# Hybrid decoder step on one core: the final norm beside the last eight expert slots

## The reference

```python
def rmsnorm(x, w):
    y = x * lax.rsqrt(jnp.mean(x * x, axis=-1, keepdims=True) + NORM_EPS)
    return y * w

# gsel = best group of the token, top_i = its two best experts in the group
eid = gsel[..., None] * EXPERTS_PER_GROUP + top_i
gate = jnp.sum(jax.nn.one_hot(eid, N_EXPERTS) * tw[..., None], axis=-2)
for e in range(N_EXPERTS):
    he = jax.nn.silu(h @ p['expert_w_gate'][e]) * (h @ p['expert_w_up'][e])
    y = y + gate[..., e:e + 1] * (he @ p['expert_w_down'][e])
x = x + y
# after the layer
y_prompt, y_sample = rmsnorm(x, norm_final)
```

## Time and profile before

| | us |
|---|---|
| median of three runs (lowest, highest) | 1233.64 (1231.39, 1235.2) |
| the profiled execution | 1233.92 |
| its span, first to last instruction | 1232.2 |
| TensorE busy | 1162.6 (94%) |
| POOL busy | 567.2 (46%) |
| DVE busy | 525.3 (43%) |
| ACT busy | 336.9 (27%) |

### The profile page before, as it was taken

The page is one execution under the profiler, slowest core; times in us unless marked ns, Lnnn a source line. Parts: engine busy times, 40 slices in busy tenths (PEclk is TensorE's granted clock), DMA queues, the critical chain, the costliest instruction groups (busy, mean ns, idle before and its releaser), DMA issues. The chain is left out here.

```text
span 1232.2 us, 31435 instructions
## 1 busy us (share of the span) xinstructions
PE 1162.6 (94%) x12690; PEld 830.3 (67%) x12690; DVE 525.3 (43%) x1250; ACT 336.9 (27%) x785; POOL 567.2 (46%) x821
## 2 busy tenths in 40 slices
PE   7999999999999999999999999689999999999990
PEld 6788878756656677787754545367777777777760
DVE  5466986644394425645523113532222222222223
ACT  5002012352441244564433222201111111111114
POOL 7512221110750248788632021046666666666661
PEclk9999999999999999999999999899999999999995
DMA  7401120134104110000075214499999897998838
GB/s 214 103 1 36 36 69 18 36 103 117 48 19 95 51 21 17 23 16 17 20 240 186 82 69 137 131 357 374 317 373 341 256 373 238 290 374 254 274 51 298
DMA packets 142874, 187.12 MB, mean 152 GB/s; under 512 B 39464, under 2 KB 89247, under 8 KB 142778
## 3 DMA queue, kind: packets, MB, share of 16 engines
q1 hardware_dynamic: 126010, 164.87, 39.6%
q0 software_dynamic: 15936, 20.57, 8.0%
q10 hardware_dynamic: 832, 0.33, 0.1%
HBM read 156.41 MB, written 29.32 MB: 151 GB/s over the span
## 5 line engine op out<-in xcount | busy, mean ns | idle before, releaser
L526 PE MATMUL ps<-hT,w_in 128*128 128x352 f32 (+1 forms) x624 | 192.6, 464 | 1.8 <-ACT cb L816 1.2
L526 PEld LDWEIGHTS ps<-hT,w_in 128*128 128x128 f32 x624 | 116.4, 190 | 66.5 <-issue 4.1
L3129 POOL DMA_INDIRECT sum_rows<-slot_out,scatter_rows x76 | 121.9, 1604 | 38.9 <-POOL scatter_rows L3128 26.1
L3261 DVE TENSOR_TENSOR slot_T<-slot_raw_T,vecs 128x256 f32<-128x256 f32 x75 | 32.8, 438 | 209.4 <-PE ps L3174 208.2
L3174 PE MATMUL ps<-qkv,slot_T 128*32 128x256 f32 x1920 | 109.9, 379 | 3.7 <-DVE slot_T L3261 2.5
L3174 PEld LDWEIGHTS ps<-qkv,slot_T 128*32 128x32 f32 x1920 | 74.8, 110 | 32.9 <-DVE slot_T L3261 4.8
L3106 POOL DMA_INDIRECT gathered<-h_rows,gather_rows x79 | 83.5, 1057 | 19.3 <-issue 12.2
L3218 ACT ACTIVATE slot_silu<-ps 128x128 f32<-128x128 f32 x77 | 21.5, 279 | 223.7 <-PE ps L3174 221.5
L3174 PE MATMUL ps<-cb,slot_T 128*32 128x256 f32 x1408 | 80.6, 379 | 0.0
L3174 PEld LDWEIGHTS ps<-cb,slot_T 128*32 128x32 f32 x1408 | 55.4, 110 | 20.5
L3224 ACT ACTIVATE slot_out<-ps,slot_weights 128x256 f32<-128x256 f32 x76 | 36.1, 475 | 112.6 <-PE ps L3185 112.6
(11 more groups left out here) (765 smaller groups left out, 2369.7 us busy)
## 6 DMA issues: line engine op xcount, KB each, us to landing
qkv<-in_expert_w_gate SPq DMA_DIRECT2D x6, 2048.0 KB
qkv<-in_expert_w_up SPq DMA_DIRECT2D x6, 2048.0 KB
qkv<-in_expert_w_down SPq DMA_DIRECT2D x6, 2048.0 KB
cb<-in_expert_w_gate SPq DMA_DIRECT2D x5, 2048.0 KB
cb<-in_expert_w_up SPq DMA_DIRECT2D x5, 2048.0 KB
zg<-in_expert_w_down SPq DMA_DIRECT2D x5, 2048.0 KB
third_w_down<-in_expert_w_down SPq DMA_DIRECT2D x5, 2048.0 KB
w_in<-in_w_in SPq DMA_DIRECT2D x18, 512.0 KB, 5.1
```

Of the source, the lines that this page charges most:

```text
L526: last = pe.matmul(pbank(b)[:, c, 0:n], w[:, k, :], hT[:, k, c * CH:c * CH + n], start=(k == 0), stop=(k == KD - 1))
L3129: pool.indirect_dma_start(quarter_sums, bass.IndirectOffsetOnAxis(ap=sidx[:, r:r + 1], axis=0), y[r][:], None, compute_op=ALU.add).then_in ...
L3261: dve.tensor_tensor(xT[:], xr[:], bc(nf, 2, ROWS_SLOT), ALU.mult).then_inc(s.xT, 1)
```

## The change

- The slots are split into early ones and the **last eight** (`LATE`). In this input these are slots 68 to 75, of which 74 and 75 hold no token. They all belong to the last four experts, one of each group, so that no token is in two of them.
- Early slots work as before. When all their adds have landed, SP loads the nine tiles of `sum_rows` (into buffers of their own, one of them the constants' masks), and ACT, POOL, DVE and SP norm and store them while the last slots are computed. The order is written out slot by slot: `ahead` and `behind` for ACT, `norms_ahead` and `norms_behind` for DVE.
- The scale of a row is computed by POOL, as (mean square + eps) to the power -0.5 (`scale`), and no longer by ACT with logarithm and exponential. ACT keeps the silu's table.
- The results of the last eight slots aren't added in DRAM. ACT evicts each as before, and SP moves its four quarters with four plain on-chip transfers into token rows (`to_rows`; tiles `last_out_0` and `last_out_1`, four slots each). POOL gathers the sums so far of these tokens (`sums`), POOL and DVE add them (`add_sums`), they are normed, and POOL writes them with indirect DMAs over the rows of `y_prompt` and `y_sample` (`last_out`, `last_sample_out`), after the plain stores of the tiles have landed.
- The token numbers for these transfers are computed by DVE ahead of its loop over slots (new L3436 to L3441).
- The norm's weights are loaded behind the third expert's. TensorE has 20 warm-up products in place of 16. The routing writes three numbers of rounds in place of six.

The core of the diff:

```diff
+                    for c in range(4):
+                        sp.dma_start(last_y[i // RING][c4[i % RING], c * QD:c * QD + QD], y[i % RING][c4[c]]).then_inc(moved[i], 16)
+                to_rows(0)
+                to_rows(1)
+                store(NT)
+                to_rows(2)
+                store(0)
+                store(1)
+                store(2)
+                to_rows(3)
+                store(3)
+                store(4)
+                store(5)
+                to_rows(4)
+                store(6)
+                to_rows(5)
+                to_rows(6)
+                to_rows(7)
+                store(7)
...
+                def scale(t):
+                    pool.wait_ge(f.sq, nth[t])
+                    pool.tensor_scalar(mean[:, t:t + 1], mean[:, t:t + 1], NORM_EPS, None, ALU.add).then_inc(f.eps, 1)
+                    pool.wait_ge(f.eps, nth[t])
+                    pool.tensor_tensor(rstd[:, t:t + 1], mean[:, t:t + 1], minus_half[:], ALU.pow).then_inc(f.rstd, 1)
...
+                scale(4)
+                pool.wait_ge(f.o0, 16)
+                sums(1)
+                pool.wait_ge(f.o1, 16)
+                sums(0)
+                last_rows(first + RING + 3, 3, n + 2)
+                scale(5)
+                scale(6)
+                scale(7)
+                add_sums(0)
+                scale(TILES)
+                pool.wait_ge(f.norm, 1)
+                pool.wait_ge(f.os, 16)
+                last_sample_out(0)
...
+                pool.wait_ge(f.out, 16 * (NT - 3))
+                last_out(0)
+                scale(TILES + 1)
+                pool.wait_ge(f.norm, 2)
+                last_out(1)
+                last_sample_out(1)
+                pool.wait_ge(f.late, 16 * 4)
...
+                ahead = {2: (1,), 3: (4,), 4: (7,)}
+                behind = {1: (NT, 0), 2: (2, 3), 3: (5, 6), 7: (TILES, TILES + 1)}
+                for i in range(LATE):
+                    if i < LATE - 1:
+                        silu(first + i + 1, hidden=True)
+                    for t in ahead.get(i, ()):
+                        mean_square(t)
+                    last_rows(i, first + i, n)
+                    for t in behind.get(i, ()):
+                        mean_square(t)
...
+                for i in range(LATE):
+                    dve.tensor_scalar(row_f[c4[i % RING], i // RING:i // RING + 1], route.token[c4[0], ds(first + i, 1)], 0.25, None, ALU.mult)
...
+                norms_ahead = {3: (NT,), 4: (2,), 5: (5,)}
+                norms_behind = {3: (0, 1), 4: (3, 4), 5: (6,), 6: (7,)}
```

More of the change, by code:

```diff
@@ L62 @@
 MOE_SEMS = "g0 g1 g2 d0 d1 d2 r0 r1 r2 r3 st ix xg xTp xT gu silu he hT down acc y0 y1 y2 y3".split()
-FIN_SEMS = "w x0 x1 x2 x3 x4 x5 x6 x7 x8 ones rstd y out".split()
+FIN_SEMS = "w x0 x1 x2 x3 x4 x5 x6 x7 x8 idx part0 part1 sum sq eps rstd y norm o0 o1 o2 os out late m0 m1 m2 m3 m4 m5 m6 m7".split()
 GATE_PE = {"columns": 1, "transposes": 2, "sums": 3, "rows": 4}
@@ L3087, in _ @@
                 sp.wait_ge(s.xg, 1)
-                for j in range(2, NE):
+                load(2)
+                sp.dma_start(wrow[:], A["norm_final"].partition_broadcast(P)).then_inc(f.w, 16)
+                for j in range(3, NE):
                     load(j)
-                landed = [sp.value_load(route.first[0:1, NE + 4 + r:NE + 5 + r], min_val=32 * NE // RING, max_val=16 * SLOTS // RING) for r in range(RING)]
-                sp.wait_ge(s.gu, bound(sp, NE - 2))
-                sp.dma_start(wrow, A["norm_final"].partition_broadcast(P)).then_inc(f.w, 16)
+                landed = early_landed(sp)
@@ L3101, in _, with store @@
-                sp.wait_ge(f.out, 16 * TILES)
+                    sp.wait_ge(out_y[r], landed)
+                for t in [NT] + list(range(NT)):
+                    sp.dma_start(tile_of[t], sum_rows[t * P:t * P + (P if t < NT else NS), :]).then_inc(x_in[t], 16)
+                first = early_slots(sp)
+                def store(t):
+                    sp.wait_ge(f.y, nth[t])
+                    dst = O["y_prompt"][0, t * P:t * P + P, :] if t < NT else O["y_sample"].rearrange("b t d -> (b t) d")
+                    sp.dma_start(dst, tile_of[t]).then_inc(stored_of(t), 16)
@@ L3103, in _ @@
+                sp.wait_ge(f.out, 16 * (NT - 3))
+                sp.wait_ge(f.late, 16 * 4)
             @block.gpsimd
```

219 lines of the change are left out of this document (149 added, 70 removed).

## The result

The changed kernel takes 1235.72 us, median of 20 runs (1233.43 to 1238.83); the kernel before took 1232.36 in 20 runs on the same chip. The ratio is 1.0021, 95% interval 1.0011 to 1.003. The forecast was 1227 and faster. The difference is within the 0.3% that the forecast took for no change, the time above its range of 1221.5 to 1235. None of these runs was in a slow state; the ratio is a little under that of the two medians, 1.0027.

What follows compares the result with a forecast made beforehand. TensorE bounds the kernel until the last expert slot, then a serial tail of 31.9 us. Span end 1223.2, plus 1.9 at the start and 1.72 beyond the span, gives 1226.8, said as 1227, against 1233.92; range 1221.5 to 1235.

Steps and rivals of the forecast that it cites:

- Loads, squares, norms beside the slots at no cost: Slots 68 to 75: the early tiles' loads, squares and norms fit into the engines' gaps; cost zero.
- The last product held up by norm 5: Last down product on TensorE: waits behind DVE's norm 5 for POOL's scale, 4.2 us late, the largest new cost.
- That product lasts 1.93 us: TensorE's last down product: keeps the earlier trace's 1.93 us, running from 1202.5 to 1204.4.
- Twelve issues of 0.43 us, 5.2 in all: SP's list behind ACT's last real output: three groups of four row moves, 0.43 us each, 5.2 us.
- From the scatter of the first half to the last scatter, 4.4 us: Tail from 1214.7 to 1219.1: POOL's scatter 1.06, scale 0.8, norm 1.3, two scatters at 1.06 us.
- From the last scatter to the end, 4.1 us: End of the span: scatters issued by 1219.1, down at 1222.8, 0.4 us for the last waits, end 1223.2.
- its own signs of being wrong: TensorE gaps in slots 69 to 72, POOL's power over 1 us, or last product to end not near 19 us.
- The start, +1.9: Between third row transpose and slot loop: DVE's added one-column instructions and drains cost 1.2 to 2.6 us, taken as 1.9.
- Warm-up at zero: Ahead of the first slots: the four added warm-up products run while TensorE waits for rows; cost zero.
- POOL and DVE get in each other's way: Rival: POOL's one-column instructions wait for whole norms at three scales, up to 3.7 us: 1230.5; chance 0.15.
- Slow power: Rival: POOL's power makes scales slow in slots 71, 72 and the tail; at 3 us each, 1239; chance 0.10.
- Late tiles: Rival: slot 67's scatter lands late, loads start 7.3 us later, TensorE loses 5.9: 1232.9; chance 0.12 including queue.

Runs made afterwards that it cites:

- e1: The changed kernel without POOL's closing wait for the four late scatters to land; ratio 1.0008 to the kernel before.
- e3: The changed kernel with DVE computing the late slots' token numbers before the first slot's rows arrive; ratio 1.0001 to the kernel before.
- e6: The changed kernel with 16 warm-up products instead of 20; ratio 1.002 to the kernel before.
- e9: The changed kernel without POOL's last two scatters and the waits for them; run once, stage length 422.9 us against 426.7.
- e12: The changed kernel with one added drain behind POOL's last gather, where POOL is idle; ratio 0.9999 to the kernel before.
- e2: The changed kernel with norm 5 moved behind slot 73's transposes; ratio 1.0015 to the kernel before.
- e10: e8 with an added drain behind POOL's last gather; ratio 0.9946 to the kernel before.
- e8: The changed kernel with the edits of e1, e2, e3 and e6, stores 5 and 7 reordered, slot 75's moves on ACT; ratio 0.9971 to the kernel before.
- e4: The changed kernel with two of the four row moves of slots 73 to 75 issued from ACT's queue; ratio 1.0019 to the kernel before.
- e11: e8 with ACT's moves ahead of its square and POOL's second-half scale ahead of its first-half scatter; ratio 0.9952 to the kernel before.
- e5: The changed kernel with a drain added behind POOL's last scale, ahead of the last scatters; run once, stage length 424.9 us against 426.7.
- e13: e8 with both the drain of e10 and the edits of e11; 1225.29 us, ratio 0.9934 to the kernel before.

## Why the prediction was wrong

It said 7.1 us less, and that the span would end at 1223.2 + 1.9 = 1225.1; it ended at 1233.1, 8.0 later. The steps in order, each against its own number:

- *Loads, squares, norms beside the slots at no cost*: right. TensorE lost 0.26 us up to slot 73's gate products; the down product behind them comes 0.5 us late. One tile landed too late for its square, by 1.18 us, and the slack took it.
- *The last product held up by norm 5*: right in place and cause. It started at 1204.23, where the forecast has 1204.4, but that closeness is partly luck: counted from the stage's start it is 397.9 us against 396.8. The hold-up is 5.6 us instead of 4.2 in this trace, and 4.6 in seven others with the same order (e1, e3 to e6, e9, e12). The store of tile 0 was issued 386.6 us into the stage (1192.94), behind SP's moves of slot 70; the forecast, with the start's 1.9, has even the store of tile 1 at 385.8. The forecast also took 0.48 us from the transpose to TensorE's start, but that pause in the earlier trace rows was ended by ACT's eviction; here it is 0.11 us (1204.12 to 1204.23).
- *That product lasts 1.93 us*: mis-sized. The price is from a row in which TensorE had waited 0.85 us ahead of it. Behind 6.42 us of waiting the products took 3.64, at the granted clock of 0.50: +1.7 us. e2, with 1.17 us of waiting and a granted clock of 1.00, shows 1.93.
- *Twelve issues of 0.43 us, 5.2 in all*: mis-sized. From the first issue to store 7 it is 1216.23 - 1208.68 = 7.55 us, 0.6 each: +2.35. The row it was from was a transfer of 16 KB. The range had 0.6 as its upper end, from loads of 512 KB. e2 shows that the end follows this list and not TensorE's last product. Eight of the twelve issues move the rows of slots 74 and 75, which hold no token in this input; a list without them was not tried.
- *Store 7 lands in 4.3 us*: 3.8 until POOL went on, -0.5.
- *From the scatter of the first half to the last scatter, 4.4 us*: 1225.41 - 1219.99 = 5.4, +1.0. The scale took 0.9 (forecast 0.8); the rest is pauses of 0.3 to 0.8 us between engines.
- *From the last scatter to the end, 4.1 us*: 7.7, +3.6. **This is the step that failed.** The forecast had 3.7 for the landing and "0.4 us for the last waits". The landing took 2.3, and then came POOL's closing drain of 5.0 us, which has no term in the sum and no place in the range. e1's trace shows that it stands on the path, e12 and e10 that taking most of it off gives 2.7 and 3.1 us.

Together 1.7 + 2.35 - 0.5 + 1.0 + 3.6 = 8.15 us from the last product on, and 0.2 less for its start gives the 8.0. Counted from the stage's start the miss is 9.3 us (426.7 against 417.5): there the product is 1.1 us late, because the start cost less than forecast and the hold-up more, and the 1.27 us by which this execution reached the stage earlier hide it.

Of its own signs of being wrong one came: from the end of TensorE's last product to the end of the span it is 25.2 us (1207.87 to 1233.1), not near 19.

With 0.4 us in the place of the drain's 5.0 the time would be some 4.6 us lower, near 1231 and inside the range. But that is not yet the gain that was forecast: e12, which takes 4.5 us of drain away, has a ratio of 0.9999 to the kernel before, no change. The drain is why the change ended slower; that it would not have paid 7.1 us even so is due to the slow last product, the list of issues and the pauses of the tail.

- *The start, +1.9*: right for DVE, whose pause grew by 1.75, although no row had the prices of a register address or a drain. Too large for TensorE: slot 71's down product starts 383.9 us into the stage, before the change 382.7. The third slot's rows reached DVE 0.4 us earlier in the stage (13.7 against 14.1) and made up for that much. TensorE does pause in the first slots, in both kernels, for these rows.
- *Warm-up at zero*: right as the kernel stands, but for another reason. The 20 products did not fit into TensorE's wait for rows: they took 7.35 us and ended at 813.8, the first slot's rows were ready at 812.5. e6 shows that DVE's later pause covers this. With the token numbers moved, it may count: e8 has slot 71's down product 382.1 us into the stage, e3 383.0, one trace each.

Of the rivals, *POOL and DVE get in each other's way* was real and small. POOL's one-column addition takes 0.22 us alone and 1.32 whenever a norm (1.28) has started beside it, and the reverse is seen once, both in this timeline of the changed kernel:

```profile
1190.45 1.28 DVE L3414 SCALAR_TENSOR_TENSOR last_sums<-last_sums,row_scales,norm_final_rows 128x1024 f32<-128x1024 f32 x1 [1.37 <-POOL row_scales L3201]
...
1190.50 1.32 POOL L3199 TENSOR_SCALAR row_mean_squares<-row_mean_squares 128x1 f32<-128x1 f32 x1
...
1207.67 2.34 POOL L3207 TENSOR_TENSOR last_out<-last_out,last_sums 128x1024 f32<-128x1024 f32 x1 [0.98 <-DMA last_sums<-sum_rows,last_rows]
...
1208.11 2.19 DVE L3393 TENSOR_TENSOR slot_T<-slot_raw_T,vecs 128x256 f32<-128x256 f32 x1 [2.15 <-PEq L3317]
```

DVE's 256-element product took 2.19 us instead of 0.42 beside POOL's sum over 1024 columns of 2.34. The Trainium skill has this as a rule (SBUF — State Buffer, section "SBUF: two separate sides"): the port pair that the two engines share is an exclusive lock, and whichever starts first holds it for its whole instruction. The trace agrees, 1.32 us beside 1.28 and 2.19 beside 2.34. It did not set the time: scale 5 and those of the late rows, on which the tail waits, ran free of it (0.22 to 0.23 us), and DVE's long product delays only a padding slot's rows. *Slow power* is refuted (0.57 us for the power). *Late tiles* did not decide here: one landed 1.18 us late for its square, and the slack took it.

## What to carry to other kernels

Ask of each engine's list how it ends: which engine does the last work, and what its closing costs when nothing runs beside it. Work that moves to another engine at the very end moves that engine's drain onto the path as well; a drain at an idle place earlier takes most of it away. Price issues by the trace row whose shape is nearest and keep the dearer one for a list that stands on the path, and after moving work off the path, sum both branches that meet in the last transfer before pricing a gain on one.

## What the runs showed of the hardware

- POOL's closing drain: 5.0 us long where POOL waits for its scatters first (changed kernel, e2, e3, e4, e6). Where it doesn't (e1, e8, e11) the drain ends 5.0 us after the last scatter's end. It is 4.9 us long without the last two scatters (e9) and 0.2 with another drain ahead of those two scatters (e5). With a drain 40 to 50 us earlier it is 0.5 us long behind the wait (e12), or ends 1.6 us after the last scatter's end where that wait is gone (e10, e13). What the 5 us are paid for is open: something POOL did up to the end of the expert loop, most of it. The kernel before had 2.5 us at its own, 7 us after POOL's last scatter had been issued; whether time or the power instruction makes the difference was not tried.
- A quarter move of 32 KB between two on-chip tiles costs SP 0.6 us of issuing in these lists, and 0.92 when ACT issues such moves beside it (1208.30 to 1213.84 for six, e4).
- The same 32 products took 1.93 us behind a wait of up to 1.2 us (before, e2, e8, e10, e11, e13; granted clock 1.00 in the first two) and 3.2 to 3.6 behind waits of 5.5 to 6.4 (the changed kernel, e1, e3 to e6, e9, e12; granted clock 0.50 in the changed kernel). The length of the wait alone does not tell: 64 gate products behind 2.57 us took 5.35 us in e1, and behind 2.82 us 3.66 in e9.
